# A hybrid attention/SSM decoder layer: x comes transposed from the host, and the row norm moves behind the first products

## The reference

```python
h = rms_norm(x, g_mix[l])            # x * rsqrt(mean(x*x) + 1e-6) * gain, per token
z = h @ w_in[l]
q, k, v, u, gate_a, gate_s = jnp.split(z, SPLIT_POINTS, axis=-1)
a = dilated_attention(q, k, v, g_q[l], g_k[l])
y = s5_ssm(u, lambda_re[l], ..., c_im[l], d_skip[l])
y = jax.nn.gelu(y)
s_out = (y @ w_glu_a[l]) * jax.nn.sigmoid(y @ w_glu_b[l])
mix = jax.nn.sigmoid(gate_a) * (a @ w_attn_proj[l]) + jax.nn.sigmoid(gate_s) * s_out
x = x + mix @ w_out[l]
h2 = rms_norm(x, g_ffn[l])
x = x + (jax.nn.silu(h2 @ w_ffn_gate[l]) * (h2 @ w_ffn_up[l])) @ w_ffn_down[l]
```

## Time and profile before

| | |
|---|---|
| median of 3 runs | 950.15 us (948.74 to 951.02) |
| the profiled execution, own time | 953.08 us |
| its span, first to last instruction | 951.4 us |
| mean granted TensorE clock | 0.987 |
| PE busy | 914.7 us (96%) |
| DVE, ACT, POOL busy | 401.5, 361.1, 184.1 us |

### The profile page before, as it was taken

How to read it: one execution, slowest core, us unless ns; L and a number is a source line. 1 busy time by engine, 2 the same in 40 slices (tenths; PEclk the granted TensorE clock), 3 DMA queues, 4 the chain that set the end, 5 groups by cost and what they waited for, 6 DMA issues and landing times.

```text
span 951.4 us, 13041 instructions
## 1 busy us (share of the span) xinstructions
PE 914.7 (96%) x4488; PEld 756.9 (80%) x4488; DVE 401.5 (42%) x554; ACT 361.1 (38%) x531; POOL 184.1 (19%) x247
## 2 busy tenths in 40 slices
PE   5999599999998999999999998999999999999998
PEld 4878488888886888888888786888888888788886
DVE  5345325557842333333267535322323323333334
ACT  5322124434442736455533234333443333322221
POOL 3399978410020101010332002000000000000000
PEclk8999989999999999999999999999999999999999
DMA  6394413844445433331442522233233232222212
GB/s 236 111 177 142 146 46 98 185 153 139 167 134 173 154 115 105 119 113 44 127 143 89 198 90 67 89 91 108 88 102 96 88 110 88 89 88 108 91 66 89
DMA packets 86590, 110.91 MB, mean 117 GB/s; under 512 B 11552, under 2 KB 52688, under 8 KB 86560
## 3 DMA queue, kind: packets, MB, share of 16 engines
q1 hardware_dynamic: 79904, 96.34, 32.2%
q0 software_dynamic: 3488, 7.89, 3.7%
q10 hardware_dynamic: 3168, 6.29, 1.8%
HBM read 94.42 MB, written 16.06 MB: 116 GB/s over the span
## 4 chain that ended last, share of the span: by engine, by line
PE 81%; POOL 9%; DVE 4%; DMA 2%; SPq 2%; issue 1%; ACT 1%; POOLq 0%; ACTq 0%; DVEq 0%
PE ps L1138 33%; PE ps L1369 25%; PE ps L1384 12%; POOL early L421 8%; PE ps L1278 3%; PE ps L1252 2%; PE ps L1255 1%; PE ps L1264 1%; SPq L344 1%; PE ps L1310 1%; DMA late<-z_d 1%; DMA early<-in_x 1%; PE ps L1205 1%; DVE late L1120 1%; DVE w_lo L581 1%
## 5 line engine op out<-in xcount | busy, mean ns | idle before, releaser
L581 DVE TENSOR_TENSOR w_lo<-w_raw,w_hi 128x1024 fp32r<-128x1024 f32 x142 | 192.7, 1357 | 366.9 <-ACT w_hi L575 366.8
L575 ACT ACTIVATE w_hi<-w_raw 128x1024 fp32r<-128x1024 f32 x142 | 150.5, 1060 | 404.5 <-PE ps L1138 162.6
L1369 PE MATMUL ps<-hT_hi,w_hi 128*128 128x512 f32 x352 | 137.6, 391 | 1.5 <-DVE hT_lo L801 1.5
L1138 PE MATMUL ps<-w_hi,hT_hi 128*128 128x512 f32 x352 | 137.5, 391 | 1.1 <-DVE w_lo L581 1.1
L1369 PE MATMUL ps<-hT_hi,w_lo 128*128 128x512 f32 x352 | 137.7, 391 | 0.0
L1369 PE MATMUL ps<-hT_lo,w_hi 128*128 128x512 f32 x352 | 137.5, 391 | 0.0
L1138 PE MATMUL ps<-w_lo,hT_hi 128*128 128x512 f32 x352 | 137.0, 389 | 0.0
L1138 PE MATMUL ps<-w_hi,hT_lo 128*128 128x512 f32 x352 | 137.0, 389 | 0.0
L421 POOL TENSOR_TENSOR early<-early 128x16 f32<-128x16 f32 (+7 forms) x137 | 112.3, 820 | 31.2 <-DVE small L833 20.5
L1369 PEld LDWEIGHTS ps<-hT_hi,w_hi 128*128 128x128 f32 x352 | 66.5, 189 | 15.5 <-issue 1.8
L1138 PEld LDWEIGHTS ps<-w_hi,hT_hi 128*128 128x128 f32 x352 | 66.1, 188 | 16.0 <-ACT early L591 1.6
(11 more groups left out here) (181 smaller groups left out, 1137.5 us busy)
## 6 DMA issues: line engine op xcount, KB each, us to landing
w_raw<-in_w_in SPq DMA_DIRECT2D x112, 256.0 KB, 3.0
w_raw<-in_w_ffn_gate SPq DMA_DIRECT2D x44, 256.0 KB, 2.8
w_raw<-in_w_ffn_up SPq DMA_DIRECT2D x44, 256.0 KB, 3.0
w_raw<-in_w_ffn_down SPq DMA_DIRECT2D x44, 256.0 KB, 2.7
z_d<-early ACTq DMA_DIRECT2D x6, 1024.0 KB, 4.4
late<-z_d SPq DMA_DIRECT2D x96, 64.0 KB
w_raw<-in_w_out SPq DMA_DIRECT2D x16, 256.0 KB, 2.9
z_d<-early SPq DMA_DIRECT2D x3, 1024.0 KB, 4.2
```

Source lines behind the costliest of these rows:

```text
L575: nc.scalar.activation(w_hi[:, j % WSPL], w_raw[:, j % WRAW], ACT.Copy).then_inc(w_hi_done, 1)
L581: nc.vector.tensor_tensor(w_lo[:, j % WSPL], w_raw[:, j % WRAW], w_hi[:, j % WSPL].bitcast(F32), ALU.subtract).then_inc(w_lo_done, 1)
L1138: ins = T.matmul(ps[:, m], lhsT, rhs, start=first and h == 0 and k == 0, stop=last and h == 1 and k == 2)
L1369: ins = T.matmul(ps[:, m], (w_hi, w_lo)[b][:, j % WSPL, at_w:at_w + P], h_acts[a][:, 2 * j + h, :], start=j == 0 and h == 0 and k == 0, st ...
```

## The change

The host also gives x transposed (`xt`, features on partitions, contiguous in each partition); the norm factor is no longer applied to x. ACT and DVE split xt times gain straight from SBUF (L617 and L834 of the changed file). PE starts with the first chunk of v (`W_V0`), then u, then the other two chunks of v: again 16 steps. The squares of all of x (L610) are summed over the 8 feature tiles by POOL (five additions), then over partitions by PE with a matrix of ones, once with tokens on partitions (`norm_row`, 128 x 4, bank 6) and once with tokens along the free axis, repeated on all partitions (`norm_all`, 128 x 512, bank 7). DVE adds eps (L859, L862), POOL raises both to -0.5. Chunks with tokens on partitions are multiplied by `norm_row` when they are emptied; u and the gates, with tokens along the free axis, by `norm_all`. For the gates DVE now empties the banks (L1042) and ACT makes the sigmoid in SBUF (L746).

```diff
@@ sync
+            sp.dma_start(small[:, 0:SMALL - 1], t["small"]).then_inc(gains_in, 16)
+            for j in range(4):
+                sp.dma_start(xt[:, 2 * j:2 * j + 2], t["xt"][:, 2 * j:2 * j + 2]).then_inc(xt_loaded[j], 16)
+                load(W_V0 + j, j, in_cols(6))
             pin = lambda dst, src: sp.dma_start(dst, src).then_inc(params_in, 16)
...
+            for c in range(1, 3):
                 for j in range(4):
                     load(W_V + 4 * c + j, j, in_cols(c + 6))
+                if c == 1:
+                    sp.wait_ge(dve_evac, DE_U + 2)
+                    sp.dma_start(u_d.rearrange("(m p) j c -> p m (j c)", p=P), uT).then_inc(u_stored, 16)
...
                 store_z(sp, c + 5, (c + 1) % 2)
@@ gpsimd
-            for n in range(TB):
-                pool.wait_ge(sumsq_done, n + 1)
-                row_root(n)
+            for half in range(2):
+                at = half * 2048
+                pool.wait_ge(sq_done, half + 1)
+                tt(sq[:, at:at + 1024], sq[:, at:at + 1024], sq[:, at + 1024:at + 2048], ALU.add)
+                tt(sq[:, at:at + 512], sq[:, at:at + 512], sq[:, at + 512:at + 1024], ALU.add)
+            pool.tensor_tensor(sq[:, 0:512], sq[:, 0:512], sq[:, 2048:2560], ALU.add).then_inc(sq_sum, 1)
+            tab(pool.memset(bb_f, 0.0))
+            pool.wait_ge(norm_eps, 1)
+            pool.tensor_tensor(norm_row[:, :], norm_row[:, :], minus_half[:, 0:1].to_broadcast([P, TB]), ALU.pow
+                               ).then_inc(norm_done, 1)
+            pool.wait_ge(norm_eps, 2)
+            pool.tensor_tensor(norm_all[:, :], norm_all[:, :], minus_half[:, 0:1].to_broadcast([P, SEQ]), ALU.pow
+                               ).then_inc(norm_done, 1)
             tab(pool.memset(toep_f, 0.0))
@@ scalar
+            act.wait_ge(gains_in, 16)
+            for j in range(4):
+                act.wait_ge(xt_loaded[j], 16)
+                for k in (2 * j, 2 * j + 1):
+                    nc.scalar.activation(hT_hi[:, k], xt[:, k], ACT.Copy, scale=gmixT[:, k:k + 1]).then_inc(hT_hi_done, 1)
+                if j < 2:
+                    hi(W_V0 + j, j)
+                if j % 2:
+                    squares(j // 2)
...
                     for m in range(4):
-                        evac(gate[:, bass.ds(i * 4 + m, 1)].rearrange("p b c -> p (b c)"), m, W_GATE + 3 + 4 * i, ACT.Sigmoid)
+                        g = gate[:, bass.ds(i * 4 + m, 1)].rearrange("p b c -> p (b c)")
+                        act.wait_ge(dve_evac, DE_Z + m + 1 + 4 * i)
+                        nc.scalar.activation(g, g, ACT.Sigmoid).then_inc(act_evac, 1)
@@ vector
+            dve.wait_ge(norm_sums, 1)
+            V.tensor_scalar(norm_row[:, :], ps[:, 6, 0:2 * TB].rearrange("p (n e) -> p n e", e=2)[:, :, 0], 1.0 / DM, EPS,
+                            ALU.mult, ALU.add).then_inc(norm_eps, 1)
+            dve.wait_ge(norm_sums, 2)
+            V.tensor_scalar(norm_all[:, :], ps[:, 7], 1.0 / DM, EPS, ALU.mult, ALU.add).then_inc(norm_eps, 1)
+            lo(W_U, 0)
+            dve.wait_ge(norm_done, 2)
             for m in (1, 3):
...
+                evac_rows(zs[:, 0, m], m, W_V0 + 3)
+            for j in range(1, 5):
+                lo(W_U + j, j)
...
+                    for m in range(4):
+                        dve.wait_ge(gemm_steps, 4 * (W_GATE + 3) + m + 1 + 16 * i)
+                        V.tensor_tensor(gate[:, bass.ds(i * 4 + m, 1)].rearrange("p b c -> p (b c)"), ps[:, m],
+                                        norm_all[:, :], ALU.mult).then_inc(dve_evac, 1)
@@ tensor
+            v0 = columns(W_V0, 4, by_token, h_acts, lambda m: None, gained_rows)
+            for _ in range(13):
+                next(v0)
+            pe.wait_ge(sq_sum, 1)
+            for n in range(TB):
+                ins = T.matmul(ps[:, 6, 2 * n:2 * n + 2], sq[:, n * P:(n + 1) * P], ones[:, 0:2], start=True, stop=True)
+            ins.then_inc(norm_sums, 1)
+            T.matmul(ps[:, 7], ones[:, :], sq[:, 0:SEQ], start=True, stop=True).then_inc(norm_sums, 1)
+            run(v0)
...
+            run(columns(W_U, 4, by_feature, h_acts, sums_read, None, 4))
...
             pe.wait_ge(pool_tab, TAB["ca"])
```

More of the change, by code:

```diff
@@ L50 @@
 OW = HD + 2
-W_U = 0
-W_V = W_U + 4
+W_V0 = 0
+W_U = 4
+W_V = 4
 W_QK = W_V + 12
@@ L591, in evac, with evac_rows, squares, gained @@
                 nc.scalar.activation(out, ps[:, m], func).then_inc(act_evac, 1)
[L593 to L599, removed]
+            def evac_rows(out, m, w_last):
+                act.wait_ge(gemm_steps, 4 * w_last + m + 1)
+                nc.scalar.activation(out, ps[:, m], ACT.Copy, scale=norm_row[:, m:m + 1]).then_inc(act_evac, 1)
+            def squares(half):
+                nc.scalar.activation(sq[:, half * 2048:half * 2048 + 2048], x_in_f[:, half * 2048:half * 2048 + 2048],
+                                     ACT.Square).then_inc(sq_done, 1)
+            act.wait_ge(gains_in, 16)
+            for j in range(4):
+                act.wait_ge(xt_loaded[j], 16)
[5 more added lines that the diff above has]
+                    squares(j // 2)
+            def gained(g):
                 for k in range(KT):
-                    act.wait_ge(x_turned, KT * wave + k + 1)
+                    act.wait_ge(x_turned, k + 1)
                     nc.scalar.activation(hT_hi[:, k], ps[:, k], ACT.Copy, scale=g[:, k:k + 1]).then_inc(hT_hi_done, 1)
[L604 to L608, removed]
+            hi(W_V0 + 2, 2)
             act.wait_ge(params_in, PARAMS)
@@ L803, in turn_lo, with evac_rows @@
                                            ).then_inc(hT_lo_done, 1)
-            def evac(out, m, w_last):
+            def evac_rows(out, m, w_last):
                 dve.wait_ge(gemm_steps, 4 * w_last + m + 1)
[L807 to L816, removed]
+                V.tensor_scalar(out, ps[:, m], norm_row[:, m:m + 1], None, ALU.mult).then_inc(dve_evac, 1)
+            dve.wait_ge(gains_in, 16)
+            for j in range(4):
+                for k in (2 * j, 2 * j + 1):
+                    dve.wait_ge(hT_hi_done, k + 1)
+                    V.scalar_tensor_tensor(out=hT_lo[:, k], in0=xt[:, k], scalar=gmixT[:, k:k + 1],
+                                           in1=hT_hi[:, k].bitcast(F32), op0=ALU.mult, op1=ALU.subtract
+                                           ).then_inc(hT_lo_done, 1)
+                if j < 3:
+                    lo(W_V0 + j, j)
             dve.wait_ge(act_tab, 1)
@@ L1124, in _, with products @@
             T = nc.tensor
-            def products(w, j, first, last, operands, bank_free, ready=None):
+            def products(w, j, first, last, operands, bank_free, ready=None, bank0=0):
                 for m in range(4):
@@ L1193, in alternating @@
                 return free
-            with pe.Fori(0, 3) as c:
-                run(columns(W_V + 4 * c, 4, by_token, h_acts, alternating(2 * c, 2 * c)))
+            for c in range(1, 3):
+                run(columns(W_V + 4 * c, 4, by_token, h_acts, alternating(2 * c - 2, 0 if c == 1 else DE_U + 2)))
             pe.wait_ge(pool_tab, TAB["ca"])
             pe.wait_ge(misc_act, MA_C)
+            pe.wait_ge(ident_in, 16)
+            pe.wait_ge(dve_evac, DE_U + 2)
             for f in range(8):
@@ L1334, in _ @@
             run(columns(w + 2, 2, by_feature, y_acts, by_act(AE_G)))
[L1335 removed]
+            run(columns(w + 4, 2, by_feature, y_acts, by_dve(DE_G)))
             glu = columns(w + 6, 2, by_feature, y_acts, by_act(AE_G + 4))
```

144 lines of the change are left out of this document (67 added, 77 removed).

## The result

The changed kernel takes 1042.82 us (median of 4 runs, 1041.08 to 1042.87) against 949.92 (4 runs, 948.74 to 951.02): a ratio of 1.097, 95% interval 1.0955 to 1.0993. It is 92.9 us slower. I had forecast 24 us slower; the time lies close to the halfway point of the rival whose power isn't overlapped between columns (X = 90, 1041).

What follows compares the result with a forecast made beforehand. POOL's chain was taken to bound the first 120 us, PE the rest. Power 23 us, less 1.9 for the chain's earlier start, plus 3.0 for gates, gave 24.1 us more: 974 us, range 951 to 1090.

Steps and rivals of the forecast that it cites:

- the rival whose power isn't overlapped between columns: POOL's power on norm_all: every column costs 0.365 us, + 188, 1138 us; chance 0.24 for a power above 60 us.
- X: Cost of POOL's power instruction on the 512 columns of norm_all, ahead of the table chain; taken as 23 us.
- What bounds the first 120 us: Up to the tables, POOL's chain of 83.1 us is the bound, and PE has 10.6 us of slack.
- the 0.365: What a power on POOL adds, in us, to a plain addition of one column: 0.553 against 0.188.
- the ends of 1.27 and 187: Bounds in us for the power on norm_all: plain arithmetic's price per column, or 0.365 paid anew by each column.
- the range: Forecast span of the kernel's time, 951 to 1090 us, the upper end meaning a power of up to 139 us.
- POOL's start: Start of POOL's table chain: at 34.9 us plus the power's length, against 36.77 before; the power may begin at 31.2.
- The chain is unchanged: POOL's table chain, up to PE's transposes, was taken to keep its length of 83.1 us.
- What waits for the power: PE stops in the u steps for about the power's length, then about 6 us for weights; a 15 us margin hides both.
- Gates: DVE emptying gate banks: hidden at three inner boundaries, 3.0 us of new PE stall ahead of W_MIX after the last pair.
- At nothing: PSUM copies that now multiply by a column, u's four copies on DVE and the FFN: no change in cost.

Runs made afterwards that it cites:

- e1_mult: The changed kernel with the power on the 512 columns of norm_all replaced by a plain product: 961.85 us.
- e9_sp: The changed kernel with norm_all made without a wide power, gates mended and table chain earlier, plus one weight step loaded ahead of u's store: 953.14 us.
- e10_tables: The kernel before with DVE's and ACT's small vectors for the tables moved ahead of weight steps W_U + 2 and W_U + 3: 939.64 us.
- e11_idle: The kernel before with a power of 512 columns, on numbers nobody reads, added on POOL behind its two memsets: 1002.38 us.
- e3_gates: The kernel before with the gates' part of the change alone, DVE copying out the banks and ACT making the sigmoid in SBUF: 957.96 us.
- e8_place: The kernel before with the transposed x as a further input, 16 columns of it loaded and not used: 954.29 us.
- e4_diag: The changed kernel with norm_all made from norm_row by diagonal blocks and a matmul with ones, POOL raising 4 columns only: 961.11 us.

## Why the prediction was wrong

*What bounds the first 120 us: right.* POOL's chain and not PE does. e1_mult, e9_sp and e10_tables show it from three sides: a shorter instruction on POOL comes off one for one (80.9 and 81.0 us), 11 us on PE's side bring 0.5 at the transposes, 10.1 on POOL's bring 9.5.

*X, the failed step.* The term of the sum that was mis-sized is the power of 512 columns: 23 us taken, 82.85 measured. That misses by 59.9 us, most of the 68.8 between the forecast and the measured difference. The row of one column (0.553) could be split in two ways, into a fixed part and a price per column; I put an eighth of the 0.365 on the column. The runs show 0.161 per column, 44% of it, and 0.204 fixed beyond a plain instruction. The choice of "an eighth" had no row behind it; the reason given for it, that many columns overlap where one can't, is what failed. 512 columns cost 512 times the price of one column, and the fixed part once. The rival without overlap had this mechanism and too high a price, 0.365. That the time is 2 us from its halfway point is luck: nothing but the middle between two prices stood behind X = 90. In the trace of before, the ends of 1.27 and 187 were all that could be had; the measured value lies inside, and the range held the time. The plain reading of the rule on additions that the prediction quoted from the Trainium skill, "GPSIMD Engine Reference", section 3.1, would have been further off (an estimated 1.3). The 4.72 us by which the prediction called that rule confirmed is a mean of instructions of 3.88 to 5.53, DVE's share in them included.

*POOL's start: nearly right.* The chain began at 119.89; 34.9 + 82.85 gives 117.8, 2.1 less. PE's first product was at 10.20 and not 8.9, because ACT loads its table only when the first piece of x is there (1.28 us from 4.91 on), and PE came to the sums at 30.77, 2.3 us later than worked out.

*The chain is unchanged: wrong by 3.2 us.* It took 79.8 us against 83.1, which I hadn't thought of as something that could move. e11_idle and the rows beside it show why it can: its length depends on which subtractions of DVE meet it. The twelve largest instructions took 1.0 us less here, and the two small ones that had met a subtraction took 0.29 and 0.58 in place of 1.30 and 1.65.

*What waits for the power: right.* PE stood in the u steps for 76.7 us, for 7.2 for weights behind the reload of u (I had 6), and for 9.9 ahead of the transposes, where I had about 15. None of it entered the sum, as said.

*Gates: right in mechanism and size,* 3.25 us against 3.0, hidden at the inner boundaries; the lower clock behind the stall, some 1.6 us, was left out. e3_gates puts the whole part at 5.0 us.

*At nothing: wrong by 5.1 us, the clock included.* Behind the tables the kernel lost 8.1 us and not 3.0. The loads of the first pair came later: PE waited 5.6 us for them, against 2.9. This wait is 4.9 to 7.2 us in all seven kernels with the change and up to 3.8 in the five without it (before 2.9, e3_gates 2.6, e8_place 3.8, e11_idle 1.5, and none in e10_tables); of these five, e8_place has the further input. Its cause stays open; that it is the place of the tensors in device memory was tried once in e8_place and neither shown nor excluded. A wait for `w_lo` ahead of W_OUT, 1.3 us here, is at most 0.2 in the trace of before and 0.9 to 2.3 in all ten experiments, those with nothing of the change included, so it can't be put down to the change, and its cause wasn't settled either.

In numbers, on the traces: the chain starts 83.1 us later, is 3.2 shorter, and 8.1 are lost behind it, which is the 88.0 us. From the forecast's side: 24.1, plus 59.9 for X, 2.1 for POOL's start, 5.1 behind the tables, less 3.2 in the chain, again 88.0. The two profiled executions stood 3.2 above (953.08) and 1.7 below (1041.08) their medians, which makes 92.9 of it.

## What to carry to other kernels

Ask first which engine's chain ends a stage. An earlier first matmul was worth nothing here (8.6 us of it, in a stage where PE had 10.6 us of slack), and the whole gain of 10 us of e10_tables lay in starting POOL's chain earlier, by moving two weight steps behind the small vectors on ACT and DVE. And an operation of which the trace shows only one column has a price per column that no argument replaces: a power of four columns in a short run, 1.03 us against 0.553, gives 0.16 us a column and with it the answer. A factor per token that is needed along both axes is better raised as 4 columns and spread by a matmul with a diagonal block (e4_diag, 961.11 us) than raised again as 512 (1042.82).

## What the runs showed of the hardware

A power on GpSimd cost 0.39 us and 0.161 us per column of 128 partitions, from 1 to 512 columns of f32; a plain two-input instruction of 512 columns cost 1.27 us in the kernel before. On ones the power of 512 columns cost 81.94 instead of 82.85. A two-input instruction of GpSimd on 2048 columns took 3.9 us with no subtraction of DVE beside it and 4.76 where one met it. DVE's subtraction of 1024 columns, with both inputs in SBUF, took 1.2 us alone and up to 4.3 us beside such instructions in the kernel before, up to 5.5 in the changed one, so each made the other wait. Behind a stall of PE of 3.25 us the granted clock was at 0.50 for some 3 us, and then full again.
